# Order of the expert products in a decoder step: gate and up of the next pair ahead of the down product

## The chip, the cores and the metric

The kernel runs on one NeuronCore of a Trainium2 chip. The metric is the device time of one execution in microseconds (us), lower is better. Everything is float32.

## The reference

One inference step of a small decoder layer for 512 prompt tokens and 32 sample tokens (544 in all, width 1024): a projection, two kinds of sparse attention, a merge, and then a mixture of experts. The change touches the last part alone, in which each token goes to 2 of 32 experts (of one group of eight):

```python
def moe_dispatch(x, idx, wts, w_gate, w_up, w_down):
    # slots: the tokens sorted by expert, each expert padded to whole blocks
    def run(args):
        t, e = args
        xb = x_pad[t]
        hdn = jax.nn.silu(xb @ w_gate[e]) * (xb @ w_up[e])
        return hdn @ w_down[e]
    yb = lax.map(run, (slot_t.reshape(n_blk, MOE_BLK), blk_e))
    y = jax.ops.segment_sum(yb.reshape(P, D) * slot_w[:, None], slot_t, num_segments=N + 1)[:N]
```

Here `w_gate` and `w_up` are 1024x256 and `w_down` 256x1024 for each expert, 3 MB of weights per expert and 96 MB for all 32.

## The kernel before

The stage `experts` begins at about 754 us. VectorE, TensorE and ScalarE first choose experts and build two lists of rows (to about 773 us). Then the experts go in pairs: pair p holds experts 2p and 2p+1, with up to 64 tokens each, so the two fill 128 rows. `LAST` is 15: pairs 0 to 14 are written out one after the other, and a loop read from a register (it makes one turn here) does the pair 15 and whatever blocks overflow. After it comes a final stage that adds the two expert rows of every token, normalises and stores.

What a pair needs, engine by engine (each engine runs its own list in order, semaphores join them):

- TensorE (PE): `turn_tokens(p)` transposes the gathered token rows, 8 of 128x128, into banks 0 and 1. `gate_up(p)` is 32 matmuls in two halves q = 0, 1, each of which waits for its weights and raises `gu_done`; it writes bank 2. `turn_hidden(p)` transposes the 128x256 hidden rows (2) into bank 3. `down(p)` is 16 matmuls into banks 4/5 or 6/7 and raises `y_done`. The profile calls them by their lines: L2346, L2357, L2367, L2379.
- VectorE (DVE): `keep_tokens` copies banks 0 and 1 to `xT` (L2560, "obT"; two slots) and raises `xT_kept`, for which `gate_up` waits; `hidden(p)` makes the two products of silu (L2565, L2567), `hid_ready`, and copies the turned hidden rows to `hidT` (L2569, one slot), `hT_kept`.
- ScalarE (ACT), for each p in this order: wait for `gu_done` of p, the sigmoid (L2414), wait for `y_done` of p, copy of the pair's result from its banks (L2418, "branch_w"), `y_ready`.
- GpSimd (POOL), for each p: wait until the tokens of p are turned, issue the gather of the tokens of pair p+2 (L2283, "oaT<-h_rows"; two slots); wait for `y_ready` of p, issue the scatter of the result rows of p (L2287). So the gather for pair p+3 stands right behind the scatter of pair p in its list.
- SyncE (SP) issues the weights of pairs 3 to 14 in this order: gate and up of p, first half, then second half (L2140, four 512 KB transfers each), each behind `gu_done` of pair p-3, then down of p (L2148, two of 1 MB) behind `y_done` of pair p-3. There are three slots for each kind of weights. The pair 15 follows in the same manner in the loop; its down load waits also for the arrival of its first half.

```python
# ScalarE, not touched by the change
            for p in range(LAST):
                act.wait_ge(gu_done, 2 * p + 2)
                sigmoid()
                if p >= 2:
                    act.wait_ge(y_stored[p % 2], 16 * (p // 2))
                keep(p, y_done, p + 1)
# GpSimd, not touched by the change
            for p in range(LAST):
                if p + 2 <= LAST:
                    pool.wait_ge(xT_done, p + 1)
                    gather(p + 2, ids[:, 0, p + 2:p + 3])
                pool.wait_ge(y_ready, p + 1)
                scatter(p, ids[:, 1, p:p + 1])
```

Of the kernel before, what the change touches and what calls it, by code (L numbers as in the profile page):

```python
# [176 lines left out]
def const(s, name, rows=P):  # L177
    a, n = AT[name]
    return s.consts[0:rows, a:a + n]
# [1935 lines left out]
NGU, NWD = 3, 3  # L2115
LAST = NE // 2 - 1
# [9 lines left out]
def down_at(s, p):  # L2126
    at, m = p % NWD, 2 * KF * D
    first = (NGU - 1) * 2 * KD * 2 * DE
    w = (s.early[:, first:first + m], s.uT[:, :, :].rearrange("p k r -> p (k r)")[:, 0:m], s.gates[:, 0:m])[at]
    return w.rearrange("p (u f n) -> p u f n", u=2, f=KF)  # L2130
# [21 lines left out]
def experts(nc, s, a, o):  # L2152
# [4 lines left out]
    with ExitStack() as ctx:  # L2157
# [3 lines left out]
        def sem(name):  # L2161
            return nc.alloc_semaphore(name)
# [43 lines left out]
        y_done, down_free = sem("ex_y_done"), sem("ex_down_free")  # L2206
# [30 lines left out]
        def half(u):  # L2237
            return slice(u * BLK, (u + 1) * BLK)
# [81 lines left out]
        def _(pe):  # L2320
# [22 lines left out]
            def turn_tokens(slot, arrived):  # L2343
                pe.wait_ge(x_in[slot % 2], arrived)
                for k in range(KD):
                    last = nc.tensor.transpose(bank[:, k // 4, k % 4 * PAIR:(k % 4 + 1) * PAIR],  # L2346
                                               xg[:, slot % 2, :].rearrange("r (p k) -> r k p", k=KD)[:, k, :],
                                               const(s, "ident"))
                last.then_inc(xT_done, 1)

            def gate_up(p, slot, arrived, done):
                pe.wait_ge(xT_kept, p + 1)
                for q in range(2):
                    pe.wait_ge(s.gate_up_in[slot % NGU][q], arrived)
                    for k in range(q * KD // 2, (q + 1) * KD // 2):
                        for u in range(2):
                            last = nc.tensor.matmul(bank[half(u), 2, :].rearrange("r (c n) -> r c n", c=2),  # L2357
                                                    xT[:, slot % 2, k, half(u)],
                                                    gate_up_at(s, slot)[:, u, :, k * DE:(k + 1) * DE],
                                                    start=(k == 0), stop=(k == KD - 1))  # L2360
                    if q or slot < LAST:
                        last.then_inc(done, 1)

            def turn_hidden(p):
                pe.wait_ge(hid_ready, p + 1)
                for f in range(KF):
                    last = nc.tensor.transpose(bank[:, 3, f * PAIR:(f + 1) * PAIR],  # L2367
                                               hid.rearrange("r (p f) -> r f p", f=KF)[:, f, :], const(s, "ident"))
                last.then_inc(hT_done, 1)

            def down(p, slot, arrived, copied, done):
                pe.wait_ge(s.down_in[slot % NWD], arrived)
                if copied is not None:
                    pe.wait_ge(y_ready, copied)
                pe.wait_ge(hT_kept, p + 1)
                for n in range(2):
                    for f in range(KF):
                        for u in range(2):
                            last = nc.tensor.matmul(bank[half(u), 4 + 2 * (slot % 2) + n, :], hidT[:, f, half(u)],  # L2379
                                                    down_at(s, slot)[:, u, f, n * 512:n * 512 + 512],  # L2380
                                                    start=(f == 0), stop=(f == KF - 1))
                last.then_inc(done, 1)

            turn_tokens(0, 16)
            for p in range(LAST):
                gate_up(p, p, 64 * (p // NGU + 1), gu_done)
                turn_tokens(p + 1, 16 * ((p + 1) // 2 + 1))
                turn_hidden(p)
                down(p, p, 32 * (p // NWD + 1), p - 1 if p >= 2 else None, y_done)
                if p == 0:  # L2390

                    pe.wait_ge(w12_ready, 1)
                    nc.tensor.matmul(bank[:, 7, 0:2], const(s, "same_row")[0:SR, :], s.w12[0:SR, :, TP],
                                     start=True, stop=True).then_inc(w12_spread, 1)
            pe.wait_ge(turns_ready, 1)
            turns = pe.value_load(nturn[0:1, 0:1], min_val=1, max_val=1 + MAXOB // 2)
            with pe.Fori(0, turns) as i:
# [47 lines left out]
        def _(dve):  # L2445
# [112 lines left out]
            def keep_tokens(p, slot):  # L2558
                dve.wait_ge(xT_done, p + 1)
                nc.vector.tensor_copy(xT[:, slot % 2, :, :].rearrange("p (b k) r -> p b (k r)", b=2), bank[:, 0:2, :])\  # L2560
                    .then_inc(xT_kept, 1)

            def hidden(p):
                dve.wait_ge(sig_ready, p + 1)
                nc.vector.tensor_tensor(sgm[:, :], sgm[:, :], bank[:, 2, 0:DE], ALU.mult).then_inc(gated, 1)  # L2565
                dve.wait_ge(gated, p + 1)
                nc.vector.tensor_tensor(hid[:, :], sgm[:, :], bank[:, 2, DE:], ALU.mult).then_inc(hid_ready, 1)  # L2567
                dve.wait_ge(hT_done, p + 1)
                nc.vector.tensor_copy(hidT[:, :, :].rearrange("p f r -> p (f r)"), bank[:, 3, 0:KF * PAIR])\  # L2569
                    .then_inc(hT_kept, 1)  # L2570

            keep_tokens(0, 0)
            for p in range(LAST):
                hidden(p)
                keep_tokens(p + 1, p + 1)
                if p == 0:
                    dve.wait_ge(w12_spread, 1)
                    link(nc.vector.tensor_copy(s.w12s[:, :], bank[:, 7, 0:2]))
            turns = dve.value_load(nturn[0:1, 0:1], min_val=1, max_val=1 + MAXOB // 2)
            with dve.Fori(0, turns) as i:  # L2580
                hidden(i + LAST)
                keep_tokens(i + (LAST + 1), LAST)

            def add(k, t):
# [68 lines left out]
```

## Time and profile before

| | us |
|---|---|
| median of 3 runs | 1060.15 (1057.28 to 1061.99) |
| profiled execution, device time | 1053.66 |
| its span in the profile | 1051.9 |
| TensorE busy | 907.5 (86%) |
| pairs of experts, first gate product to last down product | 781.0 to 1017.8 |

The span runs from the first instruction to the last; 1.8 us of the execution lie around it. Rows name the engine, the line, the operation and output <- input; "[idle before <- who]" is the time in which the engine stood still just before, and what ended it. A granted clock of 1.00 is 2.4 GHz for TensorE, 0.50 is 1.2 GHz.

### The profile page before, as it was taken

What the parts mean: (1) busy time and instruction counts of PE and PEld (TensorE: products, weight loads), DVE (VectorE), ACT (ScalarE), POOL (GpSimd) and SP (SyncE); (2) the same over time, 40 slices, a digit from 0 to 9 for tenths busy, and PEclk for the clock granted to TensorE, in tenths of its full rate; (3) what the DMA queues carried; (4) which work ended last, traced back from release to release, by engine and by line L of the source; (5) the groups of instructions that cost most, each with busy time, mean ns of one, the idle gap of its engine ahead of it and who ended that gap; (6) DMA issues with size and microseconds to landing.
All of it is one profiled execution on the core that took longest, in us unless ns stands there. A gap on an engine that the chain in (4) does not pass through costs nothing. (4 is left out here: it accounts for less than half of the span.)

```text
span 1051.9 us, 14867 instructions
## 1 busy us (share of the span) xinstructions
PE 907.5 (86%) x5957; PEld 581.6 (55%) x5957; DVE 429.8 (41%) x906; ACT 303.1 (29%) x542; POOL 198.6 (19%) x214
## 2 busy tenths in 40 slices
PE   6999998878699999989979999999659999777750
PEld 4775886555566666534669999744533444322220
DVE  4728996656428595312035422111341111111106
ACT  5435332455536776621300000011201111100002
POOL 0333330321012334423510000000111111011010
PEclk9999999899989999999989999999759999999995
DMA  9220221223267997999956550195359999999946
GB/s 327 94 92 1 94 71 43 61 61 117 85 221 261 341 372 306 356 411 354 395 185 177 184 185 21 26 341 205 109 206 395 414 413 413 414 413 414 404 167 238
DMA packets 87844, 246.87 MB, mean 235 GB/s; under 512 B 13088, under 2 KB 40928, under 8 KB 75360
## 3 DMA queue, kind: packets, MB, share of 16 engines
q1 hardware_dynamic: 66448, 144.45, 37.0%
q0 software_dynamic: 20560, 99.24, 25.0%
q10 hardware_dynamic: 768, 2.23, 0.6%
q8 instruction: 48, 0.79, 0.3%
q14 instruction: 20, 0.16, 0.0%
HBM read 238.50 MB, written 15.77 MB: 242 GB/s over the span
## 5 line engine op out<-in xcount | busy, mean ns | idle before, releaser
L1337 PEld LDWEIGHTS bank<-consts,ring 128*128 128x128 f32 x704 | 78.1, 143 | 38.6 <-ACT kT_s L1580 36.3
L1580 ACT COPY kT_s<-bank 128x1024 f32<-128x1024 f32 (+1 forms) x90 | 85.5, 996 | 45.7 <-PE bank L1337 45.7
L2357 PE MATMUL bank<-early,obT 128*64 128x512 f32 x352 | 82.0, 614 | 14.6 <-DMA early<-in_w_e_up 13.3
L1337 PE MATMUL bank<-consts,ring 128*128 128x128 f32 x704 | 89.5, 281 | 2.4 <-PEq L238 1.9
L2565 DVE TENSOR_TENSOR uT<-uT,bank 128x256 f32<-128x256 f32 x16 | 6.7, 421 | 182.2 <-ACT uT L2414 182.2
L491 POOL TENSOR_TENSOR w_lo<-w_raw,w_hi 128x512 fp32r<-128x512 f32 x37 | 49.1, 1329 | 105.0 <-ACT w_hi L534 105.0
L878 PE MATMUL bank<-w_hi,hT_hi_p 128*128 128x512 f32 x160 | 65.4, 408 | 0.0
L2357 PEld LDWEIGHTS bank<-early,obT 128*64 128x64 f32 x352 | 27.7, 141 | 66.8 <-issue 53.3
L878 PE MATMUL bank<-w_lo,hT_hi_p 128*128 128x512 f32 x160 | 62.5, 391 | 0.0
L878 PE MATMUL bank<-w_hi,hT_lo_p 128*128 128x512 f32 x160 | 62.4, 390 | 0.0
L2010 PE MATMUL bank<-w_o,uT 128*128 128x512 f32 x128 | 55.6, 593 | 2.6 <-PEq L251 2.6
L1831 PE MATMUL bank<-hT_hi,gate_w_hi 128*128 128x272 f32 x192 | 56.5, 294 | 0.0
L1831 PE MATMUL bank<-hT_hi,gate_w_lo 128*128 128x272 f32 x192 | 55.4, 288 | 0.0
L1831 PE MATMUL bank<-hT_lo,gate_w_hi 128*128 128x272 f32 x192 | 55.3, 288 | 0.0
L294 POOL DMA_INDIRECT ring<-in_cache_k_b,rows_b x32 | 30.0, 937 | 113.2 <-PE bank L1337 88.0
L2287 POOL DMA_INDIRECT expert_rows<-branch_w,ids x15 | 15.2, 1016 | 191.0 <-ACT branch_w L2418 191.0
L1860 ACT ACTIVATE sig<-bank 128x544 f32<-128x544 f32 x12 | 7.5, 625 | 138.5 <-PE bank L1831 138.5
L2414 ACT ACTIVATE uT<-bank 128x256 f32<-128x256 f32 x16 | 6.1, 383 | 139.2 <-PE bank L2357 139.2
L1104 ACT ACTIVATE prob<-bank,ntop 128x512 f32<-128x512 f32 (+3 forms) x64 | 33.1, 522 | 42.5 <-DVE ntop L1148 42.2
L1458 PE MATMUL bank<-ring,kT_s 128*32 128x512 f32 (+1 forms) x512 | 39.6, 461 | 6.2 <-DMA ring<-in_cache_v_a,rows 3.0
L2418 ACT COPY branch_w<-bank 128x1024 f32<-128x1024 f32 x16 | 16.2, 1012 | 95.7 <-PE bank L2379 95.7
L1055 PE MATMUL bank<-consts,prob 128*128 128x128 f32 x160 | 25.7, 295 | 19.2 <-ACT prob L1104 11.5
(384 smaller groups left out, 1693.8 us busy)
## 6 DMA issues: line engine op xcount, KB each, us to landing
early<-in_w_e_gate SPq DMA_DIRECT2D x44, 512.0 KB, 13.8
early<-in_w_e_up SPq DMA_DIRECT2D x44, 512.0 KB, 16.5
early<-in_w_e_down SPq DMA_DIRECT2D x12, 1024.0 KB, 13.7
w_raw<-in_w_in SPq DMA_DIRECT2D x10, 1024.0 KB, 7.4
early_gates<-in_w_e_down SPq DMA_DIRECT2D x10, 1024.0 KB, 19.0
w_o<-in_w_e_gate SPq DMA_DIRECT2D x20, 512.0 KB, 13.5
w_o<-in_w_e_up SPq DMA_DIRECT2D x20, 512.0 KB, 15.8
uT<-in_w_e_down SPq DMA_DIRECT2D x10, 1024.0 KB, 14.5
```

Source lines behind the costliest of these rows:

```text
L294: pool.indirect_dma_start(s.ring[:, r, at:at + wide], None, cache.rearrange("g (p e) h d -> (g p) (e h d)", e=e), bass.IndirectOffsetOnAxi ...
L491: nc.gpsimd.tensor_tensor(w_lo[:, k, :].bitcast(F32R), raw_w(gi, k), w_hi[:, k, :], ALU.subtract)\
L878: last = nc.tensor.matmul(bank[:, n % 4, :], l, m, start=(k == 0 and c == 0), stop=(k == KD - 1 and c == 2))
L1055: last = nc.tensor.transpose(bank[:, 4 + half, c * P:(c + 1) * P], prob[:, m % 3, half, c * P:(c + 1) * P], ident)
L1104: nc.scalar.activation(prob[:, m % 3, half, 0:width(t)], bank[:, 2 * (m % 2) + half, 0:width(t)], ACT.Exp, bias=ntop[:, m % 4, half:half + 1],
L1337: last = nc.tensor.transpose(bank[:, u, e * P:(e + 1) * P], ring[:, slot, at:at + P], ident)
L1458: last = nc.tensor.matmul(out[rows_at(u), :], probT[m][:, c * nslot + e, rows_at(u)], ring[:, slot, base + e * w:base + (e + 1) * w], star ...
L1580: nc.scalar.copy(kT[:, n % 2, u, :], bank[:, u, :]).then_inc(kT_kept, 1)
L1831: last = nc.tensor.matmul(out, l, m, start=(k == 0 and c == 0), stop=(k == KD - 1 and c == 2))
L2010: last = nc.tensor.matmul(bank[:, n % 4, :], uT[:, k, t * P:(t + 1) * P], wo[:, k, half * 512:half * 512 + 512], start=(k == 0), stop=(k = ...
L2357: last = nc.tensor.matmul(bank[half(u), 2, :].rearrange("r (c n) -> r c n", c=2), xT[:, slot % 2, k, half(u)], gate_up_at(s, slot)[:, u, : ...
L2418: nc.scalar.copy(y[:, slot % 2, :].rearrange("p (b n) -> p b n", b=2), bank[:, 4 + 2 * (slot % 2):6 + 2 * (slot % 2), :]).then_inc(y_ready, 1)
```

## The change

TensorE's list and VectorE's list are put in another order; no instruction is added or taken away. TensorE multiplies gate and up of pair p and turns the tokens of pair p+1, and only then makes the down product of pair p-1; the hidden rows of p are turned behind that. The small spread product of the sample weights moves from the turn p = 0 to p = 1. VectorE copies the tokens of p+1 ahead of the hidden rows of p. ScalarE, GpSimd and SyncE keep their lists.

```diff
+            def down_of(p):
+                down(p, p, 32 * (p // NWD + 1), p - 1 if p >= 2 else None, y_done)
+
             turn_tokens(0, 16)
             for p in range(LAST):
                 gate_up(p, p, 64 * (p // NGU + 1), gu_done)
                 turn_tokens(p + 1, 16 * ((p + 1) // 2 + 1))
-                turn_hidden(p)
-                down(p, p, 32 * (p // NWD + 1), p - 1 if p >= 2 else None, y_done)
-                if p == 0:
+                if p >= 1:
+                    down_of(p - 1)
+                if p == 1:
 
                     pe.wait_ge(w12_ready, 1)
                     nc.tensor.matmul(bank[:, 7, 0:2], const(s, "same_row")[0:SR, :], s.w12[0:SR, :, TP],
                                      start=True, stop=True).then_inc(w12_spread, 1)
+                turn_hidden(p)
+            down_of(LAST - 1)
...
+
+            def keep_hidden(p):
                 dve.wait_ge(hT_done, p + 1)
                 nc.vector.tensor_copy(hidT[:, :, :].rearrange("p f r -> p (f r)"), bank[:, 3, 0:KF * PAIR])\
                     .then_inc(hT_kept, 1)
...
             for p in range(LAST):
                 hidden(p)
-                keep_tokens(p + 1, p + 1)
-                if p == 0:
+                if p == 1:
                     dve.wait_ge(w12_spread, 1)
                     link(nc.vector.tensor_copy(s.w12s[:, :], bank[:, 7, 0:2]))
+                keep_tokens(p + 1, p + 1)
+                keep_hidden(p)
             turns = dve.value_load(nturn[0:1, 0:1], min_val=1, max_val=1 + MAXOB // 2)
             with dve.Fori(0, turns) as i:
                 hidden(i + LAST)
+                keep_hidden(i + LAST)
                 keep_tokens(i + (LAST + 1), LAST)
```

TensorE's list before, from gate and up of pair 3 on (the L numbers are those above; `obT` are the turned tokens, `oaT` the gathered ones, `hT` the hidden rows; `early`, `uT`, `early_gates` are slots of weights):

```order
L2357 MATMUL bank<-early,obT 64x512 x16
L2346 MATMUL bank<-consts,oaT 128x128 x8
L2367 MATMUL bank<-consts,hT 128x128 x2
L2379 MATMUL bank<-early,hidT 64x512 x8
L2357 MATMUL bank<-early,obT 64x512 x16
L2346 MATMUL bank<-consts,oaT 128x128 x8
L2367 MATMUL bank<-consts,hT 128x128 x2
```

The same place after the change:

```order
L2357 MATMUL bank<-early,obT 64x512 x16
L2346 MATMUL bank<-consts,oaT 128x128 x8
L2379 MATMUL bank<-early_gates,hidT 64x512 x8
L2367 MATMUL bank<-consts,hT 128x128 x2
L2357 MATMUL bank<-early,obT 64x512 x16
L2346 MATMUL bank<-consts,oaT 128x128 x8
L2379 MATMUL bank<-early,hidT 64x512 x8
```

The down product of pair 3 (`early,hidT`) stood ahead of gate and up of pair 4; it now stands behind them and behind the turning of the tokens of pair 5. In its old place is the down product of pair 2.

VectorE's list before, for two pairs (uT and hT are the two products of silu, hidT the turned hidden rows, obT the turned tokens):

```order
L2565 TENSOR_TENSOR uT<-uT,bank 128x256
L2567 TENSOR_TENSOR hT<-uT,bank 128x256
L2569 COPY hidT<-bank 128x256
L2560 COPY obT<-bank 128x1024
L2565 TENSOR_TENSOR uT<-uT,bank 128x256
```

And after it:

```order
L2570 TENSOR_TENSOR uT<-uT,bank 128x256
L2572 TENSOR_TENSOR hT<-uT,bank 128x256
L2565 COPY obT<-bank 128x1024
L2576 COPY hidT<-bank 128x256
L2570 TENSOR_TENSOR uT<-uT,bank 128x256
```

The copy of the tokens is now ahead of the copy of the hidden rows; both stand, as before, behind the two products.

## Rows read from the trace of the kernel before

**Rows 1.** Windows: us, busy of each engine, granted clock, DMA share, GB/s
```profile
core 0: us, PE busy (x) PEld busy (x) DVE busy (x) ACT busy (x) POOL busy (x), PEclk, DMA share, GB/s
788.00:800.00 12.00, 11.09 (x56) 4.61 (x54) 2.56 (x5) 1.40 (x2) 2.03 (x2) 1.00 1.00 359
820.00:860.00 40.00, 37.29 (x182) 16.37 (x180) 7.19 (x12) 4.19 (x6) 6.08 (x6) 1.00 1.02 412
940.00:980.00 40.00, 29.51 (x140) 11.14 (x139) 5.00 (x9) 3.17 (x5) 4.07 (x4) 1.00 1.02 413
```

**Rows 2.** Timeline of TensorE, first pairs: start, duration, line, operation, idle before
```profile
781.04 8.45 PE L2357 MATMUL bank<-early,obT 128*64 128x512 f32 x32 [1.39 <-DVE obT L2560]
789.42 1.16 PE L2346 MATMUL bank<-consts,oaT 128*128 128x128 f32 x8
...
792.00 3.65 PE L2379 MATMUL bank<-early,hidT 128*64 128x512 f32 x16 [0.61 <-DVE hidT L2569]
...
822.03 7.07 PE L2357 MATMUL bank<-early,obT 128*64 128x512 f32 x32
829.03 1.16 PE L2346 MATMUL bank<-consts,oaT 128*128 128x128 f32 x8
...
831.60 3.65 PE L2379 MATMUL bank<-early,hidT 128*64 128x512 f32 x16 [0.61 <-DVE hidT L2569]
835.05 7.07 PE L2357 MATMUL bank<-early,obT 128*64 128x512 f32 x32
```

**Rows 3.** Timeline of TensorE, later pairs and the last one
```profile
902.59 5.35 PE L2357 MATMUL bank<-early,obT 128*64 128x512 f32 x16 [2.24 <-DMA early<-in_w_e_up]
...
936.41 3.65 PE L2357 MATMUL bank<-w_o,obT 128*64 128x512 f32 x16 [1.53 <-DMA w_o<-in_w_e_up]
...
987.10 3.65 PE L2357 MATMUL bank<-w_o,obT 128*64 128x512 f32 x16 [1.46 <-DMA w_o<-in_w_e_up]
...
1012.76 0.50 PE L2367 MATMUL bank<-consts,hT 128*128 128x128 f32 x2 [1.40 <-DVE hT L2567]
1014.17 3.65 PE L2379 MATMUL bank<-early,hidT 128*64 128x512 f32 x16 [0.91 <-DMA early<-in_w_e_down]
```

**Rows 4.** Timeline of SyncE's queue: the first weights issued for pair 3
```profile
786.10 0.33 SPq L2140 DMA_DIRECT2D early<-in_w_e_gate  x1
...
795.68 1.44 SPq L2148 DMA_DIRECT2D early<-in_w_e_down  x2
```

**Rows 5.** Timeline of ScalarE: copy of the result of pair 3, sigmoid of pair 4
```profile
835.35 1.01 ACT L2418 COPY branch_w<-bank 128x1024 f32<-128x1024 f32 x1 [5.83 <-PE bank L2379]
842.16 0.38 ACT L2414 ACTIVATE uT<-bank 128x256 f32<-128x256 f32 x1 [5.79 <-PE bank L2357]
```

**Rows 6.** Timeline of VectorE, pair 4: a product, the two copies
```profile
842.57 0.42 DVE L2565 TENSOR_TENSOR uT<-uT,bank 128x256 f32<-128x256 f32 x1 [9.99 <-ACT uT L2414]
...
844.05 0.42 DVE L2569 COPY hidT<-bank 128x256 f32<-128x256 f32 x1 [0.60 <-PE bank L2367]
844.39 1.22 DVE L2560 COPY obT<-bank 128x1024 f32<-128x1024 f32 x1
```

**Rows 7.** Timeline of GpSimd: scatter of pair 3, gather for pair 6
```profile
837.16 1.00 POOL L2287 DMA_INDIRECT expert_rows<-branch_w,ids  x1 [10.69 <-ACT branch_w L2418]
838.47 1.01 POOL L2283 DMA_INDIRECT oaT<-h_rows,ids  x1 [0.30 <-issue]
```

**Rows 8.** Gathers, line L2283, to landing: all, the one at 838.47, the last
```profile
DMA to landing us min/median/max: 3.8/9.4/10.7
...
DMA to landing us min/median/max: 7.8/7.8/7.8
...
DMA to landing us min/median/max: 8.2/8.2/8.2
```

**Rows 9.** Windows of 1 us, columns as in rows 1: behind the wait at 902.59
```profile
904.00:905.00 1.00, 1.00 (x4) 0.30 (x2) 0.00 (x0) 0.00 (x0) 0.58 (x1) 0.50 0.99 410
...
907.00:908.00 1.00, 0.94 (x6) 0.06 (x2) 0.00 (x0) 0.00 (x0) 0.00 (x0) 1.00 1.00 410
```

## The prediction

> **What bounds the kernel now.** I read the windows first. From 788 us to the end of the pairs the DMA share is 1.00 or more at up to 413 GB/s [rows 1]: the stage moves the weights of pairs 3 to 15, 6.3 MB each, and that transfer has no gap from its start. Next I read TensorE's timeline. At first it runs a pair in 835.05 - 822.03 = 13.02 us [rows 2] on weights loaded earlier, and it does not wait for a DMA. From 902.59 it waits for weights [rows 3], and the pairs come (987.10 - 936.41) / 3 = 16.9 us apart. So TensorE's own 13.02 us are no bound of the end: the stream of weights is, and what counts is when each slot comes free. The two waits that the new order could fill (0.61 us ahead of the down product, and some 0.3 us ahead of the turning of the hidden rows) are worth 0.9 us a pair, and lie in the time that TensorE has to spare.
>
> **The start.** Before, the down product of pair 0 begins at 792.00 and ends at 795.65 [rows 2]; SyncE issues the down weights of pair 3 at 795.68 [rows 4], and everything else stands behind that in its list. Now gate and up of pair 1 come first, and at this one place nothing covers the way from the gate product to them: gate and up of pair 0 end at 789.49, the sigmoid and the two products take about 1.4 us (the 1.40 us wait in rows 3 is that way), the copy of the tokens 1.22 [rows 6], so they start at about 792.2. Then 7.0 us (829.03 - 822.03), 1.15 for the turned tokens, 3.65 for the down product: y_done of pair 0 at 804.0 where it was 795.65. The two halves of pair 3 are issued from 786.10 on [rows 4], one behind each half of the gate product of pair 0, and are 2.1 MB each, 5.1 us at 413 GB/s. The first 12 us window shows data moving from its start, so they are done at about 798, and the queue is empty until about 804.0 + 2: **some 8 us of the bounding transfer are lost**.
>
> **The round trip after that.** From then on I follow one down product to the next. Three chains go from y_done of p to y_done of p+1:
>
> Chain A, TensorE with ScalarE and VectorE. ScalarE's list is not changed: the sigmoid of p+1 stands behind the copy of the result of p, and that copy waits for the down product of p, which TensorE now makes behind gate and up of p+1. So hidden rows of p+1, meant to be made under the down product, begin when it has ended: 0.10 + 1.01 for the copy (835.35 is 0.10 behind the end of the product at 835.25) [rows 2, 5], then the sigmoid, 842.57 - 842.16 = 0.41 until the first product [rows 5, 6], two products 0.88, the copy of the tokens 1.22 with 0.1 around it: 3.8 us until gate and up of p+2. Plus 7.0 + 1.15 + 3.65: **15.6 us**, against 13.02. The change takes away 0.9 us of waiting and puts in 3.3.
>
> Chain B, the tokens. The gather for p+3 stands behind the scatter of p, which waits for the copy of the result of p. The gather starts 838.47 - 835.25 = 3.2 us behind the end of a down product [rows 2, 7]. It lands 9.4 us later in the median (3.8 to 10.7) [rows 8]. Before, its tokens were turned 20 us after that product, since gate and up of p+1, down of p+1 and gate and up of p+2 lay between (13.02 + 7). Now only gate and up of p+2 lie there, and the turned tokens of p+3 stand AHEAD of the down product of p+1. So 3.2 + 9.4 + 1.15 + 3.65 = **17.4, say 17.5 us**. While weights move, a gather lands after 7.8 to 10.7 us [rows 8], so a single round is between 15.8 and 18.7; the low end of all, 3.8, is from one while no weights moved.
>
> Chain C, the weights: down of p+3 is issued at y_done of p, gate and up of p+4 right behind it; their slots have long been free. The pairs took 16.9 us in the old stage [rows 3], so the weights are through 2 + 16.9 us behind y_done of p, just ahead of the next request at 17.5 + 2. The DMAs are therefore busy in nearly all of the 9.4 us of a gather, and I take the median of the loaded gathers and not the low end. B is the longest by a little, and a round is 17.5 us.
>
> On chain B the Trainium skill speaks otherwise: DMA: Bandwidth & Descriptors, section on the anatomy of one DMA on the GpSimd path, gives a fit of 2.0 us plus the bytes at 436 GB/s. For 128 rows of 4 KB that would be an estimated 3.2 us for the gather, and a chain B of 11.2; by that rule A or C would decide. The trace shows 3.8 us without other traffic, close to the fit, and 9.4 in this stage, so the measured one stands.
>
> The clock is a further load on A. After a wait of 2.24 us the granted clock was 0.50 (1.2 GHz) for some 3 us [rows 9], and sixteen matmuls took 5.35 us instead of 3.65 [rows 3]: 1.7 us. Chain A has 2.5 us of waiting, 0.5 of transposes and 0.8 of waiting in each round, so it may pay that too: 17.3 us. That is still just under B, so it costs nothing by itself, but it closes the way down: with faster gathers the round would be 17.3 and not 15.6.
>
> **The sum.** y_done of pair 0 at 804.0; twelve rounds of 17.5 lead to y_done of pair 12 at 1014.0. The gather of pair 15: 3.2 + 8.2 [rows 8] = 1025.4, gate and up of 14 end at 1024.8. Turned tokens and down of 13 to 1030.2. Then 3.8 + 0.5 (the hidden copy of 0.42 now stands behind that of the tokens) to down of 14: 1034.5, ending at 1038.15. Its gate and up of 15 (weights long there) until 1045.15, and from there 1.40 + 0.50 + 0.91 + 3.65 = 6.46 [rows 3] to the end of the last down product: 1051.6. Before, that is 1014.17 + 3.65 = 1017.8. The final stage starts from there in both. **Plus 33.8 us**: 1053.66 for the profiled execution becomes 1087.5, and 1060.15, the median, becomes 1094. That the moved spread product and its copy stand elsewhere (0.4 us once) I leave out.
>
> **The rivals.**
> 1. Gathers are no bound and the clock stays up; only the weights decide. Then the cost is the 8 us gap and the end: gate and up of 14 start at 987.10, their second half 5.0 later with its weights, and end at 995.8, now + 8; turned tokens and down of 13 at 1008.6, 4.3 us, down of 14 to 1016.5, gate and up of 15 to 1023.6, 6.46 more: 1030, plus 12 us, **1072**. It needs a gather of at most 8.5 us in nearly every round, and waits under chain A that do not lower the clock. Against it: 9.4 us already when only two pairs of requests were queued. 12%.
> 2. Rounds are longer: gathers near their maximum of 10.7, or a half clock that reaches into the turned tokens and the down product. 18.5 us a round, 12 more: plus 46, **1106**. 15%.
> 3. Something between 1 and the forecast, rounds of 16 to 17 us (1076 to 1086): 10%.
> 4. Faster: TensorE is the bound after all and the waits are filled, 0.9 us a pair over 15 pairs, minus 13.5, **1047**. It would need ScalarE's sigmoid not to wait behind the copy and a DMA share under 1 in the stage, from the point where TensorE's round exceeds the 16.9 us of the weights. Both lists and rows 1 speak against it. 3%.
>
> **How the numbers follow.** The forecast, rounds of 17 to 18 us (plus 27 to plus 41 with the start), has 60%. The range reaches from the cases between to rival 2, 1076 to 1108, and leaves out rivals 1 and 4 and the far side of 2, about 18%. About 0.5% (5 us) is what a measurement can tell here: slower 94%, the same 3%, faster 3%.
>
> **What would show it.** Right: the DMA share has a gap between about 798 and 806; down products 17 to 18 us apart from the first pairs on, with no wait for weights; ahead of the turned hidden rows a wait of about 2.5 us ended by VectorE; ahead of the turned tokens a wait ended by the gather; ScalarE's sigmoid right behind its copy. Half clock once a round. Wrong: rounds of 16.9 with waits for weights (rival 1), or the turned tokens never wait for a gather.

## The result

The changed kernel takes 1094.1 us (median of 4, 1092.58 to 1097.94), the one before 1058.72 beside it: a ratio of 1.0339, 95% interval 1.031 to 1.0368. It is 3.4% slower.

The stages ahead of the experts are the same in both kernels, and their length varies from one profiled execution to the next: the first gate product starts at 781.04 us in the profile of before, at 787.31 in that of after, and between 773.7 and 782.2 in those of the experiments. So I compare the **stretch of the pairs**, from the start of the first gate product to the end of the last down product: 236.8 us before, 274.5 after. With "round" I mean the time from the end of one down product to the end of the next.

TensorE's timeline of the changed kernel, two rounds of the middle (start, duration, line, operation, idle before; L2357 gate and up, L2346 tokens, L2379 down, L2367 hidden rows; it answers to [rows 2]):

```profile
894.47 1.16 PE L2346 MATMUL bank<-consts,oaT 128*128 128x128 f32 x8 [0.64 <-DMA oaT<-h_rows,ids]
895.56 3.65 PE L2379 MATMUL bank<-early_gates,hidT 128*64 128x512 f32 x16
901.57 0.51 PE L2367 MATMUL bank<-consts,hT 128*128 128x128 f32 x2 [2.36 <-DVE hT L2572]
902.71 8.78 PE L2357 MATMUL bank<-early,obT 128*64 128x512 f32 x32 [0.63 <-DVE obT L2565]
912.13 1.16 PE L2346 MATMUL bank<-consts,oaT 128*128 128x128 f32 x8 [0.64 <-DMA oaT<-h_rows,ids]
913.22 3.65 PE L2379 MATMUL bank<-early,hidT 128*64 128x512 f32 x16
```

A round is 913.22 - 895.56 = 17.7 us. Before, it was 13.02 at this place, and some 16.9 from pair 9 on, where the weights set it. The 0.61 us wait ahead of the down product is gone. In its place stand 2.36 us ahead of the hidden rows, 0.63 ahead of gate and up, 0.64 for the gather, and 1.7 us more in gate and up themselves (8.78 against 7.07 in [rows 2]). ScalarE and VectorE in a round of the same profile show where the 2.36 us come from:

```profile
863.48 1.01 ACT L2423 COPY branch_w<-bank 128x1024 f32<-128x1024 f32 x1 [16.30 <-PE bank L2379]
864.39 0.39 ACT L2419 ACTIVATE uT<-bank 128x256 f32<-128x256 f32 x1
...
864.81 0.42 DVE L2570 TENSOR_TENSOR uT<-uT,bank 128x256 f32<-128x256 f32 x1 [15.26 <-ACT uT L2419]
...
865.60 1.22 DVE L2565 COPY obT<-bank 128x1024 f32<-128x1024 f32 x1
```

The sigmoid has no wait of its own any more: it runs right behind the copy of the other pair's result, for which ScalarE stood idle 16.3 us. In [rows 5] sigmoid and copy had a wait each. And the windows, at the start of the stream of weights and in the middle (columns as in [rows 1]):

```profile
802.00:804.00 2.00, 2.00 (x12) 0.72 (x10) 0.00 (x0) 0.00 (x0) 0.00 (x0) 1.00 1.03 406
804.00:806.00 2.00, 2.00 (x12) 0.74 (x9) 0.00 (x0) 0.00 (x0) 0.00 (x0) 1.00 0.82 336
806.00:808.00 2.00, 2.00 (x15) 1.02 (x15) 0.00 (x0) 0.00 (x0) 0.00 (x0) 1.00 0.05 20
...
866.00:870.00 4.00, 3.57 (x10) 1.05 (x11) 1.15 (x2) 0.00 (x0) 1.31 (x2) 0.50 0.99 368
...
900.00:940.00 40.00, 30.61 (x124) 10.88 (x126) 6.93 (x12) 3.21 (x6) 6.09 (x6) 0.88 1.00 388
```

The DMAs fall idle at about 805.5 and start again at about 811, behind the request that SyncE issues at 810.33, when the down product of pair 0 has ended. Later their share is 1.00 as before, but at 388 GB/s where it was 412 and 413, and TensorE never waits for weights. The window from 866 on holds the start of the gate and up product of another round, at 866.88: the granted clock is 0.50 there. The chain that ended last has changed its members too, from SyncE's queue (10% of the span before) to the gathers. The first line is of the kernel before, the other two are of the changed one:

```profile
SPq 10%; PE 9%; DMA 4%; DVE 4%; issue 1%; ACT 0%; POOLq 0%; DVEq 0%; ACTq 0%
...
PE 11%; DMA 11%; DVE 4%; issue 2%; ACT 2%; POOL 1%; POOLq 0%; ACTq 0%; DVEq 0%
DMA oaT<-h_rows,ids 10%; PE bank L2379 5%; PE bank L2357 4%; PE bank L2346 2%; ACT branch_w L2423 1%; POOL expert_rows L2287 1%; DVE hT L2597 1%; DVE obT L2565 1%; DMA early<-expert_rows 0%; DVE hT L2612 0%; DMA expert_rows<-branch_w,row 0%; PE bank L2339 0%; PE bank L2326 0%; DVE uT L2570 0%; DVE hT L2572 0%
```

### The profile page after: what moved, and what is told of

It reads as the page before. It is cut to its first block and busy times, and to the rows that moved or that the text cites. A ratio compares the mean times of both kernels' runs of the same rounds, so it can differ in the third digit from the quotient of the medians.

```text
span 1095.9 us, 14867 instructions
## 1 busy us (share of the span) xinstructions
PE 934.6 (85%) x5957; PEld 581.8 (53%) x5957; DVE 428.5 (39%) x906; ACT 302.0 (28%) x542; POOL 199.2 (18%) x214
## 5 line engine op out<-in xcount | busy, mean ns | idle before, releaser
L2357 PE MATMUL bank<-early,obT 128*64 128x512 f32 x352 | 93.5, 692 | 6.9 <-DVE obT L2565 6.9
L2357 PEld LDWEIGHTS bank<-early,obT 128*64 128x64 f32 x352 | 28.2, 158 | 65.5 <-issue 56.3
L1458 PE MATMUL bank<-ring,kT_s 128*32 128x512 f32 (+1 forms) x512 | 42.7, 464 | 5.3 <-issue 3.8
L1860 ACT ACTIVATE sig<-bank 128x544 f32<-128x544 f32 x12 | 7.5, 625 | 142.0 <-PE bank L1831 142.0
L2357 PE MATMUL bank<-w_o,obT 128*64 128x512 f32 x160 | 43.0, 699 | 3.1 <-DVE obT L2565 3.1
L1055 PE MATMUL bank<-consts,prob 128*128 128x128 f32 x160 | 26.6, 302 | 18.5 <-ACT prob L1104 11.0
```

The costliest lines, as they stand in the source:

```text
L1458: last = nc.tensor.matmul(out[rows_at(u), :], probT[m][:, c * nslot + e, rows_at(u)], ring[:, slot, base + e * w:base + (e + 1) * w], star ...
```

## The experiments

Ratios are to the kernel before, run on the same chip beside them. Four kernels changed the lists of the engines that the change had left alone.

**Gather ahead of the scatter (e1).** In the change the gather for pair p+2 stands behind the scatter of pair p-1; here it stands behind that of p-2 and so is issued one round earlier.

```diff
                     gather(p + 2, ids[:, 0, p + 2:p + 3])
-                pool.wait_ge(y_ready, p + 1)
-                scatter(p, ids[:, 1, p:p + 1])
+                if p >= 1:
+                    pool.wait_ge(y_ready, p)
+                    scatter(p - 1, ids[:, 1, p - 1:p])
+            pool.wait_ge(y_ready, LAST)
+            scatter(LAST - 1, ids[:, 1, LAST - 1:LAST])
```

> The changed kernel, with GpSimd's list in another order: the gather for pair p+2 is issued as soon as the tokens of p are turned, ahead of the scatter of p-1 and of the wait for its result. Theory (a round is the longest of three chains; the token path at 17.5 us, TensorE with ScalarE, VectorE and its half clock at 17.3, weights at 16.9): the waits ahead of the turned tokens go, rounds fall from the 17.7 us measured to 17.1 to 17.4, and the pairs from 274.5 us to about 268; the kernel stays some 27 us above the one before. Rival (the token path is the only late chain, and the clock costs nothing): rounds of 15.6, cut off at 16.9 by the weights, some 12 to 18 us above the kernel before. Second rival (the weights are what is late even now, since the DMA share is 1.00): no change, 35 us above.

Measured: 1.0277 (1.0235 to 1.0319), pairs 263.9 us, rounds 16.8 in the mean of twelve. TensorE's timeline:

```profile
851.54 0.51 PE L2370 MATMUL bank<-consts,hT 128*128 128x128 f32 x2 [2.37 <-DVE hT L2575]
852.67 8.78 PE L2360 MATMUL bank<-w_o,obT 128*64 128x512 f32 x32 [0.63 <-DVE obT L2568]
861.39 1.16 PE L2349 MATMUL bank<-consts,oaT 128*128 128x128 f32 x8
862.48 3.65 PE L2382 MATMUL bank<-uT,hidT 128*64 128x512 f32 x16
868.49 0.51 PE L2370 MATMUL bank<-consts,hT 128*128 128x128 f32 x2 [2.36 <-DVE hT L2575]
```

The tokens wait for nothing, and the round is 868.49 - 851.54 = 16.95. One round of this profile had gate and up at full clock (7.09 us): it took 15.3. The token path was worth 0.9 us a round; the next chain stands right behind it. The rounds are a little under the 17.1 to 17.4 expected, since chain A takes 17.0 us with the half clock and not 17.3. Both rivals fall.

**Sigmoid ahead of the copy of the result (e2).**

```diff
                 act.wait_ge(gu_done, 2 * p + 2)
                 sigmoid()
-                if p >= 2:
-                    act.wait_ge(y_stored[p % 2], 16 * (p // 2))
-                keep(p, y_done, p + 1)
+                if p >= 1:
+                    if p >= 3:
+                        act.wait_ge(y_stored[(p - 1) % 2], 16 * ((p - 1) // 2))
+                    keep(p - 1, y_done, p)
+            act.wait_ge(y_stored[(LAST - 1) % 2], 16 * ((LAST - 1) // 2))
+            keep(LAST - 1, y_done, LAST)
```

> The changed kernel, with ScalarE's list in another order: the sigmoid of pair p stands ahead of the copy of the result of p-1. GpSimd is as in the change. Theory: the hidden rows are made under the tokens and the down product, the 2.4 us wait ahead of their transposes goes, but the gather lands as late as before: the same time turns up as a wait of 4 to 6 us ahead of the turned tokens, rounds stay at 17.4 to 18.5 (longer where the half clock moves into turned tokens and down product), 30 to 45 us above the kernel before. Rival (ScalarE's order is what costs): rounds of 16.9, 8 to 12 us above the kernel before.

Measured: 1.0529 (1.0482 to 1.0576), pairs 291.9 us, rounds 19.6. TensorE's timeline, then a window of the wait and one behind it:

```profile
842.26 7.09 PE L2357 MATMUL bank<-early,obT 128*64 128x512 f32 x32
854.26 1.97 PE L2346 MATMUL bank<-consts,oaT 128*128 128x128 f32 x8 [4.91 <-DMA oaT<-h_rows,ids]
856.16 4.23 PE L2379 MATMUL bank<-early,hidT 128*64 128x512 f32 x16
...
850.00:854.00 4.00, 0.00 (x0) 0.00 (x0) 0.66 (x2) 0.00 (x0) 0.00 (x0) 1.00 1.02 371
854.00:858.00 4.00, 3.74 (x14) 2.24 (x16) 1.23 (x1) 0.00 (x0) 0.00 (x0) 0.58 1.02 416
```

One wait is mended, and the kernel is slower than the change itself. The hidden rows follow the down product at once and gate and up are back at 7.09 us. But the gather lands hardly sooner (8.9 to 9.7 us, 9.6 to 10.2 in the change), the waiting is now in one piece of 4.9 us ahead of the tokens, and the half clock falls on the tokens (1.97 instead of 1.16) and on the down product (4.2 to 5.8 instead of 3.65). These two are links of the token path itself; gate and up were not. My expected 18.5 at most had been too low for that reason.

**Both (e3), and gate and up weights ahead of the down weights (e4).** e3 has the two edits above; e4 adds this to SyncE's list:

```diff
                     load_gate_up(sp, s, a, p, q)
-                sp.wait_ge(y_done, p - NWD + 1)
-                load_down(sp, s, a, p)
+                if p > NGU:
+                    sp.wait_ge(y_done, p - NWD)
+                    load_down(sp, s, a, p - 1)
+            sp.wait_ge(y_done, LAST - NWD)
+            load_down(sp, s, a, LAST - 1)
```

> The changed kernel with both new orders, of GpSimd and of ScalarE. Theory: TensorE's own chain is 12.3 us, tokens are early, so the weights decide again, rounds of 16.9 once they are behind. What is left of the loss is the gap of 8 us at the start of the stream of weights (the down weights of pair 3 wait for a down product that is now later, and all else stands behind them): 6 to 10 us above the kernel before. Rival (the new order is good once its waits are mended, TensorE does less waiting): at or below the kernel before.

> As e3_both, and SyncE issues gate and up of pair p ahead of the down weights of p-1, so that no request stands behind the late down product. Theory: the gap at the start goes, the stream of weights is as in the kernel before, and with it the time: minus 2 to plus 3 us. Even with every wait mended, the order of the products brings nothing, since the stage is set by the weights. Rival: if TensorE's waits had been worth something, 5 us or more below the kernel before.

Measured: e3 1.0052 (1.0026 to 1.0078), pairs 244.7 us; e4 1.0017 (0.9991 to 1.0043), pairs 240.7. Windows of e3:

```profile
792.00:794.00 2.00, 2.00 (x14) 1.12 (x12) 0.68 (x2) 0.38 (x1) 0.00 (x0) 1.00 0.81 328
794.00:796.00 2.00, 2.00 (x10) 0.61 (x10) 0.16 (x1) 0.00 (x0) 0.00 (x0) 1.00 0.04 16
796.00:798.00 2.00, 2.00 (x12) 0.85 (x8) 0.16 (x1) 0.46 (x1) 0.00 (x0) 1.00 0.00 0
798.00:800.00 2.00, 0.92 (x6) 0.39 (x7) 1.56 (x3) 0.56 (x1) 0.61 (x1) 1.00 0.52 164
```

The gap in the stream of weights is some 5 us here, and in e4 it is gone: DMA share 0.99 from 786 to 800 us at 361 GB/s. e3 is 244.7 - 240.7 = 4.0 us longer than e4 over the pairs and 4.4 in the medians of ten runs each, which is near the length of the gap. It isn't a clean price of the gap: the end of e4 holds 3.4 us of half clock that the end of e3 doesn't have:

```profile
958.00 3.65 PE L2385 MATMUL bank<-early_gates,hidT 128*64 128x512 f32 x16 [2.25 <-DMA early_gates<-in_w_e_down]
...
1006.99 5.35 PE L2363 MATMUL bank<-early,obT 128*64 128x512 f32 x16 [2.48 <-DMA early<-in_w_e_up]
...
1014.85 5.35 PE L2385 MATMUL bank<-early,hidT 128*64 128x512 f32 x16 [0.61 <-DVE hidT L2585]
```

In the first line TensorE waits 2.25 us and the clock stays up, in the second it waits 2.48 us and sixteen matmuls take 5.35 us instead of 3.65. This is also why the pairs of e4 take 240.7 us and not the 236.8 of before. With all three lists mended, the new order is equal to the old one within the interval of the whole time, as the bound by weights says.

**The weights taken away.** Three kernels load only the first expert of each pair from pair 3 on, one loads nothing for pairs 3 to 14; the products run on what the slots hold. Each was run once, so its whole time carries the spread of the earlier stages; I compare the stretch of the pairs and the rounds.

```diff
-    for u in range(2):
+    for u in range(2 if p < NGU else 1):
```

> The kernel before, with half of the weights: from pair 3 on only the first expert of a pair is loaded, the second multiplies what its slot held (that part of the computation is left out); products and order are the same. Theory: the stage is no longer set by weights, TensorE runs at its own 13.02 us a pair to the end, the pairs take some 198 to 202 us instead of 236.8, so 35 to 39 us less in all. Rival (something else holds the later pairs at 16.9): no change.

> The changed kernel with both new orders (GpSimd's gather ahead, ScalarE's sigmoid ahead) and half of the weights. Theory: TensorE's own chain in the new order: 7.0 + 1.15 + 3.65 + 0.5, rounds of 12.2 to 12.5 us against 13.02 in the old order, pairs about 8 to 10 us shorter than those of the kernel before with half the weights. This is what the idea of the change is worth where TensorE is the bound. Rival (gathers or ScalarE still late): rounds of 13 or more.

> The changed kernel with the same half of the weights. Theory: weights are not what is late, so the round is the longer of the token path, 8.0 us plus the landing of the gather (shorter with half the traffic, 4 to 8 us instead of 9.8), and the chain of TensorE, ScalarE and VectorE, 15.6 us, or 17.3 where the clock falls: rounds of 15.6 to 17.3, pairs of 245 to 270 us, and some 50 to 65 us behind the kernel before with half its weights. Rival (the weights are the bound of the changed kernel too): rounds fall by 3 us or more, to under 14.5.

> The changed kernel without the weights of pairs 3 to 14 (their products run on what the slots hold; that part of the computation is left out). With half of the weights a gather still landed after 10 to 11 us, at the end of the burst of weights that is issued at the same moment. Theory (a gather is late because the weights are issued together with it): now it lands after 4 to 5 us, no wait is left ahead of the turned tokens, and the round is the chain of TensorE, ScalarE and VectorE alone: 15.3 us at full clock, 17.0 with the half clock in gate and up. Rival (the gather path is slow by itself): landings of 8 us or more and rounds as before, 17.7.

| | weights | pairs, us | round, us | gather lands after, us |
|---|---|---|---|---|
| before | all | 236.8 | 13.0, later 16.9 | 7.8 to 10.7 |
| e5, before | half | 210.8 | 13.0 | 7.0 to 7.8 |
| e7, change with both lists mended | half | 201.1 | 12.1 | 9.3 to 10.6 |
| change | all | 274.5 | 17.7 | 9.6 to 10.2 |
| e6, change | half | 284.2 | 18.5 | 9.6 to 11.0 |
| e9, change | none | 266.3 | 16.8 | 4.1 to 4.2 |

(Gathers of the first and last rounds are left out.) e5 and e7 are the case for the idea: where TensorE is the bound, the new order with its other lists mended saves 9.7 us over the pairs. In e5 my expected 198 to 202 us had left out the first round; the rounds are as expected. e6 was the miss: half the bytes, and the gather is no earlier. Its windows around the gather issued at 823.98 show why:

```profile
822.00:824.00 2.00, 0.70 (x2) 0.32 (x2) 1.81 (x3) 0.12 (x1) 1.04 (x2) 0.77 0.78 299
...
830.00:832.00 2.00, 2.00 (x12) 0.70 (x10) 0.00 (x0) 0.00 (x0) 0.00 (x0) 1.00 1.02 408
832.00:834.00 2.00, 2.00 (x10) 0.42 (x6) 0.00 (x0) 0.00 (x0) 0.00 (x0) 1.00 0.42 166
834.00:836.00 2.00, 1.36 (x12) 1.14 (x12) 0.00 (x0) 0.00 (x0) 0.00 (x0) 1.00 0.00 0
...
DMA to landing us min/median/max: 10.7/10.7/10.7
```

The weights of a round come in a burst of about 11 us from 822 on, because SyncE, like GpSimd, is released by the down product. The gather goes out into that burst and lands at 834.7, just behind its end; the 6 us of idle DMAs that follow are of no use to it. In e5 the same bytes are spread over the round, and it lands after 7 to 8 us. e9 has no burst, and the gather takes 4.2 us. So the gather is late because of the burst; by what path the burst holds it up, these runs do not show. TensorE's timeline of e9:

```profile
860.65 3.65 PE L2379 MATMUL bank<-uT,hidT 128*64 128x512 f32 x16
866.67 0.50 PE L2367 MATMUL bank<-consts,hT 128*128 128x128 f32 x2 [2.36 <-DVE hT L2572]
867.81 8.78 PE L2357 MATMUL bank<-early,obT 128*64 128x512 f32 x32 [0.63 <-DVE obT L2565]
```

Its rounds, 16.8 in the mean, are those of e1, which moves all the weights: neither tokens nor weights are in that chain. So of the 4.7 us that a round of the change has lost against 13.02, 0.9 are the token path and the rest is TensorE with ScalarE, VectorE and the clock. e6 is longer than the change by 0.8 us a round, and its timeline accounts for this: the waits for the gather come to 1.65 us a round over the same twelve rounds, against 0.73 in the change. In the two longest rounds (20.7 and 20.1 us) TensorE waits 3.65 and 3.1 us for it, and the half clock falls on the down product (5.35 us) and not on gate and up.

**The clock's price (e12).** e1 with work for TensorE in the wait ahead of the hidden rows:

```diff
                     down_of(p - 1)
+                    for _ in range(14):
+                        nc.tensor.transpose(bank[:, 3, 2 * PAIR:3 * PAIR], const(s, "ident"), const(s, "ident"))
```

> As e1_gather_first (rounds 17.0, 1.028 of the kernel before), with 14 transposes of a constant behind each down product, into a part of bank 3 that nobody reads: TensorE has work in the wait of 2.4 us ahead of the hidden rows. Theory (that wait lowers the clock, which costs 1.7 us a round): gate and up take 7.1 us instead of 8.8 in every round, the first rounds take 15.3 us, later ones are held at 16.9 by the weights; 5 to 10 us less than e1_gather_first. Rival (gate and up are slow for another reason, as the weights' traffic): 8.8 us as before, and no gain.

Measured: 1.0112 (1.0071 to 1.0152), pairs 247.2 us against 263.9 of e1. TensorE's timeline:

```profile
849.76 1.58 PE L2397 MATMUL bank<-consts 128*128 128x128 f32 x13
852.04 0.50 PE L2370 MATMUL bank<-consts,hT 128*128 128x128 f32 x2 [0.69 <-DVE hT L2577]
853.17 7.09 PE L2360 MATMUL bank<-w_o,obT 128*64 128x512 f32 x32 [0.63 <-DVE obT L2570]
```

1.7 us of useless work put where 1.7 us of waiting were, and the kernel gains 16.7 us over the pairs: the matmuls of gate and up run at full clock in every round, and the rounds are 15.3 until the weights are late, from the eleventh on. This is more than the 5 to 10 us expected, since the weights took longer to become the bound than I had thought.

**One half of the change alone (e10, e11), and a wait at the end (e8).** e10 is the change with VectorE's two copies in their old order; e11 is the kernel before with only those two copies exchanged; e8 is the kernel before without the last wait of SyncE for arrived weights:

```diff
# e10
-                keep_tokens(p + 1, p + 1)
                 keep_hidden(p)
+                keep_tokens(p + 1, p + 1)
...
# e8
-                sp.wait_ge(s.gate_up_in[LAST % NGU][0], i * 64 + 64 * (LAST // NGU + 1))
                 load_down(sp, s, a, LAST, e)
```

> TensorE's new order alone: VectorE copies the hidden rows ahead of the tokens again, as in the kernel before. Theory: gate and up of the next pair wait for transposes, hidden copy and only then the copy of the tokens, about 1 us more in the chain of TensorE, ScalarE and VectorE (17.0 becomes 18 us), which then is as long as the token path or longer: rounds of 18.0 to 18.4 instead of 17.7, 3 to 8 us above the changed kernel, 38 to 44 above the one before. Rival (the copies' order matters nothing): as the changed kernel.

> VectorE's new order alone, in the kernel before: the hidden rows are copied behind the tokens, so each down product starts up to 0.8 us later. Theory: the rounds of the first pairs grow from 13.0 to about 13.8, and nothing comes of it, since the weights set the end: within 2 us of the kernel before. Rival (TensorE's time counts): 10 us or more above.

> The kernel before, with one wait taken out: the down weights of the last pair no longer wait for the arrival of the first half of its gate and up weights. Theory (the stage is the stream of weights): the DMAs, whose share falls to 0.28 between 1000 and 1003 us, stay busy, and the end comes 2 to 4 us earlier. Rival (one engine's backlog sets the arrival, the others only idle): no change within 1 us.

Measured: e10 1.0465 (1.0412 to 1.0519), pairs 286.7, rounds 18.5; e11 1.0016 (0.9981 to 1.0051), pairs 237.2, rounds of 13.5 at first and then the weights; e8 0.9998 (0.9974 to 1.0022). The wait ahead of gate and up is 1.65 us in e10 and 0.63 in the change, so TensorE's order needs VectorE's. e10 lost more than expected: in five of the twelve rounds gate and up took 9.8 to 10.1 us, half clock for longer, and the first down product came 2.4 us later than in the change, with the half clock in gate and up of pair 1 and 1 us more of waiting ahead of them. e11 shows TensorE's time as worthless in the kernel before: 0.5 us a round lost over nine rounds, nothing to be measured at the end. e8's 2 to 4 us were not there, though the DMAs now stay busy between 1000 and 1003 us (share 0.96 to 1.07, where it was 0.21 to 0.39): the idle DMAs at the end of the kernel before cost nothing that can be measured.

Nothing that was run beats the kernel before; e4 and e11 equal it.

## Why the prediction was right, step by step

| | forecast | measured in the profile |
|---|---|---|
| first gate product to first down product's end | 23.0 | 810.29 - 787.31 = 23.0 |
| twelve rounds | 12 x 17.5 = 210 | 1023.14 - 810.29 = 212.9 |
| from there to the end of the last down product | 37.6 | 1061.8 - 1023.14 = 38.7 |
| more than before, over the pairs | 33.8 | 274.5 - 236.8 = 37.7 |
| time | 1094 | 1094.1 |

- **The start.** Right in time: the first down product ends 23.0 us behind the first gate product, as forecast. The gap in the stream of weights is in its place but shorter, from about 805.5 to 811, some 5.5 us where 8 were forecast. e3 against e4 prices a gap of 5 us at about 4 us. In the change itself it cost nothing of its own, since weights are never late there; what counted was the 8.4 us in which the first down product comes later.
- **Chain B, the tokens.** Right as the longest in most rounds: TensorE waits for a gather in 10 of 13, 0.2 to 2.4 us. In two of the others (18.2 and 18.0 us) gate and up took 9.87 and 9.80 us, and chain A was the longer; the forecast had B ahead by 0.2 us only, and that B leads in the others is in part luck. The landings, 9.6 to 10.2, are a little above the 9.4 taken. The reason given, that the DMAs are busy throughout, was too coarse: e5, e6 and e9 show that the burst issued at the same moment sets it.
- **Chain A.** The waits came as worked out: 2.36 and 0.63 us, and 15.3 us a round at full clock (e1, e12) against 15.6. The clock, called a load that chain A "may pay", is paid in all but one of the twelve rounds; with it chain A is 17.0 in e1, against 17.3. The step "costs nothing by itself" holds only beside chain B; without chain B it is the largest term, as e12 shows.
- **Chain C.** Right that it is not the longest: TensorE never waits for weights in the change, and without weights (e9) the rounds are those of e1 with all of them.
- **The end.** 1.1 us short: the down product of pair 14 took 5.05 us at the half clock, 1.4 more than taken. The wait for the gather of pair 15, which the sum has, did not come; gate and up of pair 14 took 8.5 us instead.
- **Rival 1** (1072) came true only when both lists were mended, in e3, and at 6 us above before, not 12: the 4.3 us waits that its sum held at the end go too, and the gap was 5 us and not 8. **Rival 2** is e2, rounds of 19.6: the half clock in tokens and down product is real, but in the change itself it reached only one down product, that of pair 14. **Rival 3** (rounds of 16 to 17) fell with the 17.7 measured. **Rival 4** fell by e4.
- The estimate of 3.2 us for a gather, worked out from the fit of the Trainium skill (DMA: Bandwidth & Descriptors, Anatomy of one DMA), was near the 4.2 us of e9, where no weights moved, and far from the 9.6 to 10.2 in the change.

The time agrees better than the parts do: the forecast was laid on the median of 1060.15, and the run beside the change gave 1058.72, so 35.4 us are to be explained, between the 33.8 of the sum and the 37.7 of the profile.

Nearly all of the 37.7 us is lost in the first half of the stage. The first down product comes 8.4 us later, and the next eight rounds, in which TensorE set the pace before, take 142.0 us where they took 104.7. In the four after them, where weights set the pace before, the change loses 2.1 us, and from the end of down product 12 on it is 10.0 us shorter (38.7 against 48.7): gate and up of pair 13 have already been made there, and no weights are waited for.

## What to carry to other kernels

When one engine's list is reordered to look ahead, write down for every other engine what stands behind the wait that has now become longer: here ScalarE's sigmoid and GpSimd's gather each stood behind a result that came a pair later, and both had to move with it. Price the idea against the real bound first; here the weights made it worth nothing even when all lists fit, and 0.9 us a round where they did not. And price each mend by itself: of two chains of nearly equal length, the one mend gained 0.9 us a round (e1) and the other lost 1.9 (e2), because the waits collected into one longer wait on the longest chain, and the half clock moved onto it.

## What the runs showed of the hardware

- In the change, a wait of 2.4 us, 0.5 us of transposes and 0.6 us of waiting were followed by a granted clock of 0.50 in 11 of 12 rounds: gate and up took 1.3 to 2.8 us more, most often 1.7. With the first wait filled down to 0.7 us it fell in none of the rounds (e12). In e2 a wait of 4.9 us cost 0.8 us in the tokens and up to 2.2 us in the down product behind it.
- The length of one wait does not say whether the clock falls. Sixteen matmuls took 5.35 us behind waits of 2.24 us (before) and 2.1 to 2.4 us (e3), and 3.65, full clock, behind waits of 2.1 to 2.7 us ahead of down products (e4) and of 2.52 us (e12). Behind the same wait of 1.76 us for the same down weights they took 3.65 us in the kernel before and 5.35 in e8. Why the one and not the other, no run here shows.
- A gather of GpSimd of 128 rows lands after 4.1 to 4.2 us with no weights moving (e9). With half of the weights it lands after 7.0 to 7.8 us where they are spread over the round (e5), and after 9.6 to 11.0 where they are issued together with it (e6). The moment counted, and not the mean rate.
- A DMA share of 1.00 does not say that the DMAs are the bound: it was 1.00 in the change, at 388 GB/s, with no wait for weights; taking all weights away (e9) shortened the rounds by 0.9 us only, by way of the gather, to those of e1.
